# RWKV scan: the output weights' split ahead of the diagonals on GpSimd, the weights' rounding at the head's start on ScalarE

## The chip, the cores and the metric

The kernel runs on one core of one Trainium2 chip. The metric is the device time of one execution in microseconds (us). The engines are named as in the profile: PE is TensorE's matmul, PEld its weight load, DVE is VectorE, ACT is ScalarE, POOL is GpSimd, SP is SyncE, whose queue issues the loads and stores.

## What is computed

The program is a whole two-block network on 512 tokens of 1024 channels. The change lies in one part of it, the bidirectional RWKV scan of the second block, with 16 heads of 64 channels, over 256 context and 512 latent steps:

```
def _wkv_step(S, inp):
    r_t, w_t, k_t, v_t, a_t, b_t = inp
    sa = einsum('zbhvk,zbhk->zbhv', S, a_t)
    S = S * w_t[..., None, :] + sa[..., :, None] * b_t[..., None, :] + v_t[..., :, None] * k_t[..., None, :]
    return S, einsum('zbhvk,zbhk->zbhv', S, r_t)

def rwkv_out(y, h, xx, r, k_mod, v, mu, ln_g, ln_b, r_k, g1, g2, wo):
    y = layernorm(y, ln_g, ln_b, GN_EPS)                    # per head
    bonus = einsum('bthk,zbthk->bth', _heads(r) * r_k, _heads(k_mod))
    y = y + bonus[..., None] * _heads(v)
    gate = sigmoid(xg @ g1) @ g2
    return (y * gate) @ wo
```

Beside the scan proper, each head's turn of the program also does two small things for the stage that follows. It takes one 128x512 block of the output weights `wo` and splits it into a rounded part and the rest, so that the later product can be made of three products of rounded values. And it adds the bias `ln_b` of the head's 64 channels to the bonus rows (the offset).

## The kernel before, in words

`rwkv_scan` (L3304) works head by head, both directions at once, one in partitions 0 to 63 and one in 64 to 127. A head's 768 steps are cut into 12 chunks of 64 (`STEPS`), in three groups of four (`NG` = 3). Each engine has a hand-written program; `heads(body)` calls `body(h, walk, ahead)` for h = 0 to 15, in which three heads are in work at once:

- head h is *prepared*: PE multiplies the factors into pair products (`pair_set` 0 to 4, masked by DVE into `pairs`), turns the keys with the diagonals `eed` (`turn` 0 to 2, copied by ACT into `bkT`, L3560), and a triangular inverse R is grown in 15 steps (`NZ` = 15): for each n, PE makes z from `off[n]` and T, ACT copies it to Z (L3580), PE makes zr from Z and R, and DVE adds zr to R (L3737) and transposes R into T (L3706);
- head h-1 is *walked*: 12 steps, each of X (L3510), SA (L3514) and Sm (L3519), copied by ACT between PE's products; steps 0 to 2 lie at the start of the body, between pair products and turned keys, the others between the growth steps, and y is copied at the very end (L3507). `walk_solve`, PE's product of X and R, needs all 15 updates of R for step 0 and the copied X in each step;
- the *factors* of head h+1 are made, between the growth steps, by DVE (prefix scan L3624, `at_rt` L3655, `bh` L3661, `ee` L3677 at the twelfth step) and ACT, and by POOL.

**POOL** (L3456 on), in `body`: the three joins of R (L3477, after DVE's `scaled`), the fifteen `off` products (L3482), then `factors(ahead)`: `km` (L3461), `kh` (L3466, after ACT's exponential `e_neg`), the diagonals `eed` (L3468, after DVE's `ee`, semaphore `bd_ready`). Then the split `w_lo` = `w_raw` - `w_hi` (L3486, after ACT's rounding, `hi_made`) and the offset of the head before (`add_shift`, L3493).

**ACT**, in `body`: walk steps 0 and 1, the copies of the turned keys with walk step 2 between them, the copies of z with the rest of the walk and the exponentials of the factors. At n = `NZ` - 4 = 11 it rounds the weights' block, `w_hi` = `w_raw` (L3594), after `raw_loaded` (both loads of the block: 128x512 of the weights, L3421, and the head's 64 biases on 128 partitions into `shift`, L3422) and after the stores of the block before.

**DVE**, in `body`: masks, scales and eyes at the start, then the growth steps with the factor parts between them. Ahead of the last update of R (n = 14) stand the two bonus multiplies of `add_bonus` (L3726).

**SP**, in `body`: loads of the factors of the head ahead; then it waits for the copy of y of the walked head, loads v (L3415), waits for `bonus_done` and `lo_made`, stores `w_hi` and `w_lo` (L3438), waits for the offset of the head before and loads the next block's `w_raw` and `shift` (L3421, L3422):

```
                    if walk is not None:
                        sp.wait_ge(s["y_copied"], walk + 1)
                        if ahead is not None:
                            load_v(ahead)
                    sp.wait_ge(s["bonus_done"], h + 1)
                    sp.wait_ge(s["lo_made"], h + 1)
                    for d, w in zip(wo, (w_hi, w_lo)):
                        sp.dma_start(block_of(d, h), w[:].bitcast(F32)).then_inc(s["w_stored"], 16)
                    if ahead is not None:
                        if h:
                            sp.wait_ge(s["bonus_shifted"], h)
                        load_raw(ahead)
```

Of the kernel before, what the change touches and what calls it, by code (L numbers as in the profile page):

```python
# [10 lines left out]
ACT = mybir.ActivationFunctionType  # L11
# [3292 lines left out]
def rwkv_scan(nc, name, S, a, kF, rF, sgF, aF, vS, y, bonus_rows, wo):  # L3304

    NG = STEPS // 4
    NZ = LEVELS * NG
# [12 lines left out]
    with Stage(nc, name) as st:  # L3320
# [43 lines left out]
        s = {n: st.sem(n) for n in names}  # L3364
# [13 lines left out]
        def cs(x):  # L3378
            return x[:].rearrange("p (c t) -> p c t", t=CH)
# [7 lines left out]
        def heads(body):  # L3387
            for h in range(HEADS):
                body(h, h - 1 if h else None, h + 1 if h + 1 < HEADS else None)
# [6 lines left out]
        with st.block() as block:  # L3396
# [56 lines left out]
            def _(pool):  # L3453
                pool.wait_ge(s["const_loaded"], 96)

                def factors(h):  # L3456
# [7 lines left out]
                    if h:  # L3464
                        pool.wait_ge(s["tr_ready"], h * NG)
                    nc.gpsimd.tensor_tensor(kh[:], cs(km), cs(e_neg), ALU.mult).then_inc(s["kh_made"], 1)  # L3466
                    pool.wait_ge(s["bd_ready"], h + 1)
                    nc.gpsimd.tensor_tensor(eed[h % 3][:], eye[:].rearrange("p (o t) -> p o t", o=1).broadcast_to([P, STEPS - 1, CH]),  # L3468
                                            ee[h % 3][:, 0:STEPS - 1].rearrange("p (c o) -> p c o", o=1).broadcast_to([P, STEPS - 1, CH]), ALU.mult).then_inc(s["eed_made"], 1)

                def body(h, walk, ahead):
# [11 lines left out]
                    if ahead is not None:  # L3483
                        factors(ahead)
                    pool.wait_ge(s["hi_made"], h + 1)
                    nc.gpsimd.tensor_tensor(w_lo[:], w_raw[:], w_hi[:], ALU.subtract).then_inc(s["lo_made"], 1)  # L3486
                    if h:
                        add_shift(h - 1)

# [5 lines left out]

                factors(0)
                heads(body)
                add_shift(LAST)

            @block.scalar  # L3500
            def _(act):
# [47 lines left out]
                def body(h, walk, ahead):  # L3549
# [12 lines left out]
                    walk_both(0)  # L3562
                    walk_both(1)
                    copy_turned(0)
                    if walk is not None:
# [18 lines left out]
                    for n in range(NZ):  # L3584
                        if n + 1 < NZ:
                            copy_z(n + 1)
                        walk_part(walk, 2 * n)
                        walk_part(walk, 2 * n + 1)
                        if ahead is not None:
                            factor_part(ahead, n)  # L3590
                        if n == NZ - 4:
                            act.wait_ge(s["raw_loaded"], 32 * h + 32)
                            act.wait_ge(s["w_stored"], 32 * h)
                            A(w_hi[:], w_raw[:], ACT.Copy).then_inc(s["hi_made"], 1)  # L3594

# [946 lines left out]
```

## Time and profile before

| What | us |
|---|---|
| median of 3 runs | 4310.55 |
| their range | 4308.35 to 4314.49 |
| the profiled execution | 4311.74 |
| its span | 4309.8 |
| PE busy | 3577.5 (83%) |
| PEld busy | 2528.0 (59%) |
| DVE busy | 2089.9 (48%) |
| POOL busy | 1369.2 (32%) |
| ACT busy | 1244.6 (29%) |

The profiled execution is one run of the program under the hardware profiler. Its time is the device time, its span goes from the first to the last instruction. Busy time is the sum over the instructions of an engine, without waiting. The shares are those of the whole span; the scan is the part from about 2940 to 3640 us. In the lines of a timeline, the first number is the start, the second the duration, both in us, then engine, line of the program, operation, output and inputs, shapes and count; in brackets stands how long the engine was idle before, and what ended it. Instructions of one kind that follow each other are merged, and one may begin before the one ahead of it has ended. "issue" is time in which the engine waited for nothing that the profile shows.

### The profile page before, as it was taken

What the parts mean: (1) busy time and instruction counts of PE and PEld (TensorE: products, weight loads), DVE (VectorE), ACT (ScalarE), POOL (GpSimd) and SP (SyncE); (2) the same over time, 40 slices, a digit from 0 to 9 for tenths busy, and PEclk for the clock granted to TensorE, in tenths of its full rate; (3) what the DMA queues carried; (4) which work ended last, traced back from release to release, by engine and by line L of the source; (5) the groups of instructions that cost most, each with busy time, mean ns of one, the idle gap of its engine ahead of it and who ended that gap; (6) DMA issues with size and microseconds to landing.
All of it is one profiled execution on the core that took longest, in us unless ns stands there. A gap on an engine that the chain in (4) does not pass through costs nothing. (4 is left out here: it accounts for less than half of the span.)

```text
span 4309.8 us, 78120 instructions
## 1 busy us (share of the span) xinstructions
PE 3577.5 (83%) x31346; PEld 2528.0 (59%) x31346; DVE 2089.9 (48%) x3273; ACT 1244.6 (29%) x2681; POOL 1369.2 (32%) x1069
## 2 busy tenths in 40 slices
PE   8889999998999999968787848876888887587874
PEld 6667777556778887752222326635888886432221
DVE  4559963448983455640000036625878875400002
ACT  3352223443223223321111021223454443111112
POOL 4444453343443554720000023403455452000001
PEclk9999999999999999979898978997999997798997
DMA  4125532214542223449999963334223223599997
GB/s 125 47 79 178 182 133 79 63 50 150 181 161 76 98 74 120 146 179 420 421 421 421 421 244 108 125 134 130 67 64 78 53 78 113 210 394 426 426 426 298
DMA packets 245738, 819.09 MB, mean 190 GB/s; under 512 B 61336, under 2 KB 68840, under 8 KB 185680
## 3 DMA queue, kind: packets, MB, share of 16 engines
q1 hardware_dynamic: 236960, 786.13, 48.8%
q0 software_dynamic: 7920, 28.84, 1.7%
q8 instruction: 209, 3.42, 0.3%
q14 instruction: 73, 0.60, 0.0%
q10 hardware_dynamic: 576, 0.09, 0.0%
HBM read 738.84 MB, written 76.12 MB: 189 GB/s over the span
## 5 line engine op out<-in xcount | busy, mean ns | idle before, releaser
L2810 POOL DMA_INDIRECT moe0e_xg<-moe_h,moe_first_rows x19 | 18.0, 950 | 593.7 <-DMA moe_first_rows<-moe_table 544.0
L3758 PE MATMUL scan_bank<-scan_T,scan_off 64*64 64x64 f32 x3840 | 163.0, 223 | 43.5 <-issue 35.9
L1209 DVE SCALAR_TENSOR_TENSOR f0u_ada<-hT,condition,f0u_ada 128x512 f32<-128x512 f32 x168 | 196.9, 1242 | 0.2 <-DVE f0u_ada L1209 0.2
L1209 DVE SCALAR_TENSOR_TENSOR f1u_ada<-hT,condition,f1u_ada 128x512 f32<-128x512 f32 x168 | 191.2, 1207 | 0.2 <-DVE f1u_ada L1209 0.2
L2842 PE MATMUL moe0e_p_g<-moe_ring,moe0e_xT 128*64 128x512 f32 x608 | 175.1, 652 | 18.2 <-ACT moe0e_xT L2880 9.7
L2810 POOL DMA_INDIRECT moe1e_xg<-moe_h,moe_first_rows x16 | 15.1, 942 | 537.0 <-DMA moe_first_rows<-moe_table 454.9
L3482 POOL TENSOR_TENSOR scan_off<-scan_pairs,scan_join 128x256 f32<-128x256 f32 x240 | 181.3, 795 | 0.0
L359 POOL TENSOR_TENSOR gmi_w_lo<-gmi_rows_w,gmi_w_hi 128x512 fp32r<-128x512 f32 x64 | 120.5, 1883 | 161.6 <-ACT gmi_w_hi L399 161.6
L3758 PEld LDWEIGHTS scan_bank<-scan_T,scan_off 64*64 64x64 f32 x3840 | 140.2, 138 | 51.8 <-issue 42.8
L2842 PE MATMUL moe0e_p_u<-moe_ring,moe0e_xT 128*64 128x512 f32 x608 | 169.1, 631 | 0.0
L359 POOL TENSOR_TENSOR p_w_lo<-p_rows_w,p_w_hi 128x512 fp32r<-128x512 f32 (+3 forms) x88 | 113.4, 1290 | 163.0 <-ACT p_w_hi L399 163.0
L2909 DVE TENSOR_TENSOR moe0e_gated<-moe0e_gate,moe0e_p_u 128x512 f32<-128x512 f32 x19 | 13.1, 688 | 310.9 <-ACT moe0e_gate L2884 310.9
L3758 PE MATMUL scan_bank<-scan_R,scan_Z 64*64 64x64 f32 x3840 | 160.1, 221 | 1.8 <-issue 1.7
L1141 POOL TENSOR_TENSOR f1u_w_lo<-f1u_w,f1u_w_hi 128x1024 fp32r<-128x1024 f32 x42 | 115.5, 2769 | 136.4 <-ACT f1u_w_hi L1157 136.4
L2842 PE MATMUL moe1e_p_g<-moe_ring,moe1e_xT 128*64 128x512 f32 x512 | 145.9, 650 | 15.5 <-ACT moe1e_xT L2880 8.1
L1141 POOL TENSOR_TENSOR f0u_w_lo<-f0u_w,f0u_w_hi 128x1024 fp32r<-128x1024 f32 x42 | 114.0, 2735 | 138.2 <-ACT f0u_w_hi L1157 138.2
L2861 PE MATMUL moe0e_p_y<-moe_ring,moe0e_gatedT 128*64 128x512 f32 x608 | 140.9, 618 | 13.0 <-ACT moe0e_gatedT L2886 13.0
L3737 DVE TENSOR_TENSOR scan_R<-scan_R,scan_bank 128x256 f32<-128x256 f32 x240 | 98.2, 409 | 91.8 <-PE scan_bank L3758 90.7
L2842 PE MATMUL moe1e_p_u<-moe_ring,moe1e_xT 128*64 128x512 f32 x512 | 140.9, 630 | 0.0
L3758 PEld LDWEIGHTS scan_bank<-scan_R,scan_Z 64*64 64x64 f32 x3840 | 138.7, 137 | 2.4 <-issue 2.0
L2909 DVE TENSOR_TENSOR moe1e_gated<-moe1e_gate,moe1e_p_u 128x512 f32<-128x512 f32 x16 | 11.0, 688 | 261.0 <-ACT moe1e_gate L2884 261.0
L2861 PE MATMUL moe1e_p_y<-moe_ring,moe1e_gatedT 128*64 128x512 f32 x512 | 118.1, 615 | 11.0 <-ACT moe1e_gatedT L2886 11.0
(745 smaller groups left out, 10403.5 us busy)
## 6 DMA issues: line engine op xcount, KB each, us to landing
moe_ring<-in_moe_w_gu_dram SPq DMA_DIRECT2D x280, 1024.0 KB, 20.9
moe_ring<-in_moe_w_down_dram SPq DMA_DIRECT2D x140, 1024.0 KB, 22.6
hT<-in_ada_w_dram SPq DMA_DIRECT2D x48, 1024.0 KB, 6.6
f0u_w<-in_ffn_w_gate_up_dram SPq DMA_DIRECT2D x22, 1024.0 KB, 4.9
f1u_w<-in_ffn_w_gate_up_dram SPq DMA_DIRECT2D x22, 1024.0 KB, 4.8
gmi_rows_w<-in_ga_w_in_dram SPq DMA_DIRECT2D x64, 256.0 KB, 2.8
gmo_w<-in_ga_w_out_dram SPq DMA_DIRECT2D x64, 256.0 KB, 3.0
p_rows_w<-in_ab_w_in_dram SPq DMA_DIRECT2D x48, 256.0 KB, 2.7
```

Source lines behind the costliest of these rows:

```text
L359: nc.gpsimd.tensor_tensor(w_lo[t % 2][:, 0:width], w[t % RAW][:, 0:width], w_hi[t % 2][:, 0:width], ALU.subtract).then_inc(w_lo_made, 1)
L1141: nc.gpsimd.tensor_tensor(w_lo[u][:, g], w[:, g], w_hi[u][:, g], ALU.subtract).then_inc(lo_made, 1)
L1209: ins = V.scalar_tensor_tensor(out=acc[:, z, :], in0=src, scalar=cond[:, n * HALF + k, z:z + 1], in1=acc[:, z, :], op0=ALU.mult, op1=ALU.add)
L2810: pool.indirect_dma_start(xg[:], None, H.h, bass.IndirectOffsetOnAxis(rows[:, 0:1], 0)).then_inc(gathered, 16)
L2842: mm = nc.tensor.matmul(p[r, :], xT[:, kd, r], ring[:, s, half, k, g * HID:(g + 1) * HID], start=(kd == 0), stop=(kd == KD - 1), skip_grou ...
L2861: mm = nc.tensor.matmul(p_y[n][r, :], aT[:, kh, r], ring[:, s, half, k, n * BANK:(n + 1) * BANK], start=(kh == 0), stop=(kh == KH - 1), sk ...
L2909: nc.vector.tensor_tensor(act_in[:], sg[:], p_u[:], ALU.mult).then_inc(gated, 1)
L3482: nc.gpsimd.tensor_tensor(off[n][:], strict(u, g), over4(join[:, l + 1, :]), ALU.mult).then_inc(s["off_ready"], 1)
L3737: V.tensor_tensor(R[u][:, g4, :], R[u][:, g4, :], quad(zr_bank[n % 2]), ALU.add).then_inc(s["zr_added"], 1)
L3758: mm = nc.tensor.matmul(out[r], lhsT[r], rhs[r], start=start, stop=stop, skip_group_check=True)
```

## The change

On GpSimd, `factors` loses its last instruction, which becomes a function of its own, `diagonals`. In `body` the split and the offset now come right after `factors(ahead)`, and the diagonals after both. On ScalarE the rounding of the block, with its two waits, moves from the growth step n = 11 to the start of the body, behind walk steps 0 and 1 and ahead of the copies of the turned keys. No instruction is added or removed.

```diff
--- before.py
+++ after.py
@@ -3464,6 +3464,8 @@
                     if h:
                         pool.wait_ge(s["tr_ready"], h * NG)
                     nc.gpsimd.tensor_tensor(kh[:], cs(km), cs(e_neg), ALU.mult).then_inc(s["kh_made"], 1)
+
+                def diagonals(h):
                     pool.wait_ge(s["bd_ready"], h + 1)
                     nc.gpsimd.tensor_tensor(eed[h % 3][:], eye[:].rearrange("p (o t) -> p o t", o=1).broadcast_to([P, STEPS - 1, CH]),
                                             ee[h % 3][:, 0:STEPS - 1].rearrange("p (c o) -> p c o", o=1).broadcast_to([P, STEPS - 1, CH]), ALU.mult).then_inc(s["eed_made"], 1)
@@ -3482,10 +3484,15 @@
                         nc.gpsimd.tensor_tensor(off[n][:], strict(u, g), over4(join[:, l + 1, :]), ALU.mult).then_inc(s["off_ready"], 1)
                     if ahead is not None:
                         factors(ahead)
+                    split_block(h)
+                    if h:
+                        add_shift(h - 1)
+                    if ahead is not None:
+                        diagonals(ahead)
+
+                def split_block(h):
                     pool.wait_ge(s["hi_made"], h + 1)
                     nc.gpsimd.tensor_tensor(w_lo[:], w_raw[:], w_hi[:], ALU.subtract).then_inc(s["lo_made"], 1)
-                    if h:
-                        add_shift(h - 1)
 
                 def add_shift(h):
                     hs = slice(h * HK, h * HK + HK)
@@ -3494,6 +3501,7 @@
                                             shift[h % 2][:].rearrange("p (o c) -> p o c", o=1).broadcast_to([P, NT, HK]), ALU.add).then_inc(s["bonus_shifted"], 1)
 
                 factors(0)
+                diagonals(0)
                 heads(body)
                 add_shift(LAST)
 
@@ -3561,6 +3569,9 @@
 
                     walk_both(0)
                     walk_both(1)
+                    act.wait_ge(s["raw_loaded"], 32 * h + 32)
+                    act.wait_ge(s["w_stored"], 32 * h)
+                    A(w_hi[:], w_raw[:], ACT.Copy).then_inc(s["hi_made"], 1)
                     copy_turned(0)
                     if walk is not None:
                         walk_x(walk, 2)
@@ -3588,10 +3599,6 @@
                         walk_part(walk, 2 * n + 1)
                         if ahead is not None:
                             factor_part(ahead, n)
-                        if n == NZ - 4:
-                            act.wait_ge(s["raw_loaded"], 32 * h + 32)
-                            act.wait_ge(s["w_stored"], 32 * h)
-                            A(w_hi[:], w_raw[:], ACT.Copy).then_inc(s["hi_made"], 1)
 
                 act.wait_ge(s["const_loaded"], 96)
                 act.wait_ge(s["consts_made"], 2)
```

## Rows read from the trace of the kernel before

**Rows 1.** Stretches (us, busy of each engine with count, PEclk, DMA share, GB/s): scan, one head

```profile
core 0: us, PE busy (x) PEld busy (x) DVE busy (x) ACT busy (x) POOL busy (x), PEclk, DMA share, GB/s
2940.00:3640.00 700.00, 604.00 (x17728) 571.75 (x17728) 538.50 (x1075) 324.06 (x994) 336.09 (x369) 0.95 0.25 64
3248.73:3289.47 40.74, 36.23 (x1116) 34.45 (x1112) 33.84 (x68) 19.81 (x63) 21.19 (x23) 1.00 0.24 63
```

**Rows 2.** Timeline of PE near one head boundary (start us, us; in brackets idle before, releaser)

```profile
3235.45 0.68 PE L3758 MATMUL scan_bank<-scan_T,scan_off 64*64 64x64 f32 x16 [0.33 <-issue]
...
3243.11 0.33 PE L3758 MATMUL scan_bank<-scan_X,scan_R 64*64 64x64 f32 x4 [0.84 <-DVE scan_R L3737]
...
3250.36 0.31 PE L3758 MATMUL scan_bank<-scan_X,scan_R 64*64 64x64 f32 x4
```

**Rows 3.** Timeline of DVE, same stretch

```profile
3230.66 2.10 DVE L3655 SCALAR_TENSOR_TENSOR scan_at_rt<-scan_k,scan_negkk,scan_lw 128x384 f32<-128x384 f32 x1
...
3233.49 0.58 DVE L3655 SCALAR_TENSOR_TENSOR scan_at_rt<-scan_k,scan_negkk,scan_lw 128x384 f32<-128x384 f32 x1
3233.98 0.55 DVE L3661 TENSOR_TENSOR scan_bh<-scan_ka,scan_e_neg 128x384 f32<-128x384 f32 x1
...
3234.90 0.45 DVE L3706 STREAM_TRANSPOSE scan_T<-scan_R 128x256 f32<-128x256 f32 x1
...
3240.66 1.94 DVE L3726 TENSOR_TENSOR rw_bonus<-scan_v,scan_bonus 64x256 f32<-64x256 f32 x2
```

**Rows 4.** Instructions by tile over the kernel (ns min/median/max)

```profile
L3486 POOL TENSOR_TENSOR scan_w_lo<-scan_w_raw,scan_w_hi x16: 1267/1448/1452, 2990.3 to 3602.4; 128x512 fp32r<-128x512 f32 x16
...
L3726 DVE TENSOR_TENSOR rw_bonus<-scan_v,scan_bonus x32: 409/1050/1523, 2989.4 to 3605.0; 64x256 f32<-64x256 f32 x32
L3493 POOL TENSOR_TENSOR rw_bonus<-rw_bonus,scan_shift x16: 717/904/909, 3034.6 to 3605.5; 128x256 f32<-128x256 f32 x16
```

**Rows 5.** Timeline of POOL, same stretch

```profile
3230.52 1.82 POOL L3466 TENSOR_TENSOR scan_kh<-scan_km,scan_e_neg 128x768 f32<-128x768 f32 x1 [6.94 <-ACT scan_e_neg L3544]
3239.55 1.37 POOL L3468 TENSOR_TENSOR scan_eed<-scan_eye,scan_ee 128x704 f32<-128x704 f32 x1 [7.21 <-DVE scan_ee L3677]
3240.88 1.45 POOL L3486 TENSOR_TENSOR scan_w_lo<-scan_w_raw,scan_w_hi 128x512 fp32r<-128x512 f32 x1
3242.28 0.91 POOL L3493 TENSOR_TENSOR rw_bonus<-rw_bonus,scan_shift 128x256 f32<-128x256 f32 x1
3244.19 0.73 POOL L3477 TENSOR_TENSOR scan_R<-scan_pairs,scan_join 128x256 f32<-128x256 f32 x1 [1.00 <-DVE scan_pairs L3694]
```

**Rows 6.** Timeline of DVE in two heads, the prefix scan

```profile
3217.55 0.56 DVE L3624 TENSOR_TENSOR_SCAN scan_L<-scan_keep,scan_lw 128x192 f32<-128x192 f32 x1 [0.60 <-ACT scan_lw L3529]
...
3256.50 0.91 DVE L3624 TENSOR_TENSOR_SCAN scan_L<-scan_keep,scan_lw 128x192 f32<-128x192 f32 x1 [0.41 <-ACT scan_lw L3529]
```

**Rows 7.** Timeline of ACT, boundary of rows 2

```profile
3237.66 0.62 ACT L3594 ACTIVATE scan_w_hi<-scan_w_raw 128x512 fp32r<-128x512 f32 x1
...
3240.69 0.38 ACT L3507 ACTIVATE rw_y<-scan_bank 128x256 f32<-128x256 f32 x1 [0.43 <-PE scan_bank L3767]
...
3248.73 0.60 ACT L3560 ACTIVATE scan_bkT<-scan_bank 128x512 f32<-128x512 f32 x1 [0.71 <-PE scan_bank L3773]
```

**Rows 8.** Timeline of SyncE's queue, same boundary

```profile
3241.10 1.30 SPq L3415 DMA_DIRECT2D scan_v<-rw_v  x2
...
3244.09 0.64 SPq L3422 DMA_DIRECT2D scan_shift<-in_rw_ln_b_dram  x1
```

**Rows 9.** Landings by tile: shift over the kernel, shift here, w_raw over the kernel

```profile
DMA to landing us min/median/max: 4.4/5.2/6.7
...
DMA to landing us min/median/max: 6.3/6.3/6.3
...
DMA to landing us min/median/max: 3.4/3.8/5.3
```

**Rows 10.** Stretches of a head in which PE stood longer

```profile
3372.06:3413.98 41.92, 37.34 (x1116) 35.62 (x1112) 32.64 (x68) 20.04 (x63) 20.45 (x23) 0.96 0.29 76
3377.00:3381.00 4.00, 4.00 (x91) 4.00 (x89) 0.14 (x1) 1.69 (x6) 4.00 (x7) 0.57 0.37 96
```

**Rows 11.** Timeline of PE in that head

```profile
3376.12 0.22 PE L3849 MATMUL scan_bank<-ones,scan_rk 64*64 64x1 f32 x2 [1.67 <-issue]
```

## The prediction

> **What bounds the kernel now.** I read the stretch table first. The scan takes 700 us of the 4309.8 us span, and PE, the busiest engine, is busy for 604 of them; DVE is busy for 538.5, ACT and POOL for about half [rows 1]. No engine is full, so what counts is who waits for whom within one head, of which there are 16, some 41 us each. The profile's chain of work that ended last names only the tail of the kernel and is of no use here. I then read the timelines of all engines over one head boundary, 3230 to 3253 us, and those of the other boundaries, which repeat it.
>
> At the boundary, PE issues the product of X and R of the next walk (the first matmul that needs the last update of R) after standing 0.84 us for DVE's update of R [rows 2]. DVE is late with that update because two bonus multiplies lie in front of it and take 1.94 us together [rows 3]. The pair would need about 0.8 us (0.41 us is the shortest of the 32 [rows 4]); the rest is waiting, because POOL is at that moment in the diagonals (3239.55 to 3240.92), the split (to 3242.33) and the offset [rows 5]. A vector instruction with two SBUF operands ends only after the POOL instruction that is under way: the same shows beside POOL's kh, where DVE's first half of `at_rt` takes 2.10 us and the second half, with POOL idle, 0.58 us [rows 3, 5]. The prefix scan of 128x192 takes 0.56 us with POOL idle and 0.91 us beside the `off` products [rows 6].
>
> So the change has a real target: POOL's split and offset lie beside DVE's last two-operand work of a head, ahead of something that PE waits for.
>
> **The change, part by part.**
>
> 1. *The split and the offset leave the boundary.* They run 3240.88 to 3243.19 now [rows 5]. Without them the bonus multiplies wait for the diagonals alone, that is to about 3240.92, and end near 3241.5, 1.1 us earlier. PE can use only the 0.84 us that it stands [rows 2]. That is a gain of at most 0.84 us at each of 15 boundaries. POOL's next work, the joins of R, starts after waiting 1.00 us for DVE [rows 5], so POOL was not late for it and gains nothing of its own.
>
> 2. *They arrive right behind kh, at about 3232.3.* There POOL is idle now until 3239.55 [rows 5], so POOL's own time costs nothing, and the diagonals still wait for DVE's small product of decays. But DVE is not idle: it has the second half of `at_rt` (3233.49) and the first half of bh (3233.98), both with two SBUF operands, in between updates of R and transposes [rows 3]. When kh ends, DVE finishes the `at_rt` it was held in (3232.76), then the split runs some 1.27 us (its shortest, with DVE idle; 1.45 us beside DVE [rows 4, 5]) to about 3234.0. The second `at_rt` half is held to there and ends at 3234.45 instead of 3234.0. The offset, 0.7 us at its shortest [rows 4], runs to 3235.15, and bh, held again, ends about 1.05 us late. Behind it stand an update of R and the transpose of 3234.90. PE's growth step at 3235.45 starts 0.1 us after that transpose, having stood 0.33 us [rows 2, 3]. There is no slack there, and PE is then without a pause until the y products. I take +1.0 us a head. Bounds: 0.3 us if only the first hold counts and the second is hidden, 2.0 us (split plus offset, 1.27 + 0.7) if POOL keeps the memory over both.
>
> 3. *ScalarE's rounding leaves its old place.* There it took 0.52 us of ACT's queue (its 0.62 us, of which the next instruction overlaps some 0.1 us [rows 7]) and made the copies behind it at most some 0.15 us late. I take -0.1 us; bounds 0 and -0.5 us.
>
> 4. *The rounding in its new place waits for a load.* Only the timeline of SyncE's queue shows this term. ACT is ready for it at 3248.02: it stands 0.71 us there now, until the first turned keys come at 3248.73 [rows 7]. The rounding needs 0.5 us, so by its length alone it would fit. But it waits for both loads of its block, the weights and the offset's row. SyncE issues them at the end of a series that starts when y is copied (3240.69 to 3241.07): two loads of v, two stores of the block before, the weights' load, and at 3244.09 the load of `shift` [rows 7, 8]. That last one lands 5.2 us after its issue in the median (4.4 to 6.7 over 16), and 6.3 us in this head; the weights themselves take 3.8 us [rows 9]. So the rounding may start at 3249.3 (median) or 3250.4 (this head), 1.3 to 2.4 us after ACT is ready for it. Before, ACT asked for these loads some 30 us later, and they cost nothing. Nothing in this series becomes earlier: y's copy does not depend on the bonus, and the stores are at most a few tenths bound by it.
>
> Queued behind it on ACT are the copy of the turned keys and the copy of X of step 2. With 0.5 us for the rounding and 0.5 us for the copy, X is written at 3250.6 to 3251.7. PE takes X at 3250.36 today [rows 2]. So PE's walk is 0.3 to 1.4 us later than now, 0.85 us in the middle, even though the boundary ahead of it was 0.84 us quicker. The gain of part 1 is thus consumed: PE arrives early and stands, about 1.7 us in all.
>
> How much of 0.85 us reaches the end of the head? The profile has a natural experiment. In the head of 3372 us PE stood 1.67 us in the bonus matmuls and then ran at a granted clock of 0.57 for 4 us, half speed, together some 2.4 us of delay; that head took 41.92 us where one without such a stop took 40.74 [rows 1, 10, 11]. About half came through, since DVE then meets less of POOL's `off` work. I take 0.4 us. Bounds 0 and 1.4 us.
>
> **The sum.** 1.0 - 0.1 + 0.4 = 1.3 us a head, with part 1 already used up inside part 4. Times 15 it is 19.5 us. The first head has its load long before, and the last has no following head whose factors it prepares; neither matters. The profiled execution took 4311.74 us, 1.9 us more than its span and 1.2 us above the median of the three runs, 4310.55. So 4331 us.
>
> *A page against the rows.* The row says 5.2 us for the 32 KB of `shift` (64 floats on 128 partitions). The Trainium skill, DMA: Bandwidth & Descriptors, section on the anatomy of one DMA, fits a transfer as about 2.0 us fixed plus its bytes over 436 GB/s, an estimate by it of 2.1 us here. By that the row of `shift` would be there at 3246.2, ahead of ACT; the trace does not agree, and the trace's duration is used. The page's figure would lead to the faster rival below.
>
> **The rivals.**
>
> *Faster: the load is not what ACT waits for.* If the landing that ends the wait were at or before 3248.0, so if `shift` landed within 3.9 us of its issue, ACT's copy would move by nothing and the 0.84 us of part 1 would stay. With the holds of DVE hidden by PE's own work, 15 x 0.84 = 12.6 us are won: 4299 us. For it: the weights alone take 3.8 us. Against it: the smallest of 16 landings of `shift` is 4.4 us. It decides at 3.9 us.
>
> *About the same: the costs are the small ends.* Holds of 0.3 us and a wait that passes on 0.1 us come to 0.3 us a head, 5 us in all: 4316 us. For it: DVE does stand for PE at times, and a hold that falls on such a time is free. Against it: PE, not DVE, is the one without a pause from 3235.45 on, and a late start of its growth step is not made good.
>
> *Much slower: the clock.* PE stands about 1.7 us in part 4, as long as in the head of 3372 us, after which the granted clock was 0.57, which is the lower of its levels (1.2 of 2.4 GHz) for most of 4 us [rows 10, 11]. If that follows in most heads, another 1.2 us of half-speed work comes through: 2.5 us a head, 4349 us. Against it: over the whole scan the clock is 0.95 [rows 1], although PE stands at every boundary.
>
> *The change does not do what it says* is hardly open: the order of each queue is written by hand, and the diff moves whole instructions.
>
> **How the numbers follow.** The forecast has 0.60, the clock 0.15, the small ends 0.17, the faster one 0.08. A measurement of this kernel can tell about 0.2%, 8.6 us, from no change. Part of the small-end case reaches beyond 8.6 us. So faster 0.07, same 0.15, slower 0.78. The range from 4312 to 4349 takes in the small ends and the clock and leaves out the faster rival and what lies beyond the bounds.
>
> **What would show it.** In the changed kernel ACT should show an idle time of 2 to 3 us before the rounding, ended by a DMA, and PE an idle time of 1 to 2.5 us before the product of X and R of step 2, ended by ACT. DVE's bonus pair should fall from 1.9 to about 1.0 us, PE's 0.84 us before the first product of X and R should vanish, and DVE's second half of `at_rt` and first half of bh should grow from 0.58 and 0.55 to about 1.0 and 1.2 us. The period of a head should go from 41 to a little over 42 us. I would be wrong if ACT does not idle before the rounding, or if DVE's two instructions keep their length.

## The result and the profile after

The changed kernel takes 4320.93 us in the median of 15 runs (4314.45 to 4337.17). The kernel before, run beside it, takes 4310.09 us in the median of 15 (4299.87 to 4321.01). The ratio is 1.003, with a 95% interval of 1.0022 to 1.0038: slower by 12.9 us (9.5 to 16.4). The forecast was 20 us slower, a range from 4312 to 4349. The sign and the range hold, the size was too large. The profiled execution took 4318.85 us, with a span of 4317.0.

The stretch table of the changed kernel has the same columns as [rows 1]; its three rows are a long stretch of the scan, 4 us from the copy of X in one head boundary, and the 4 us behind those. The row below them, by itself, is the long stretch in the kernel before.

```profile
3000.00:3600.00 600.00, 528.46 (x15892) 505.35 (x15890) 465.52 (x954) 284.61 (x888) 298.78 (x329) 0.97 0.24 63
3497.00:3501.00 4.00, 3.67 (x72) 3.67 (x74) 0.16 (x1) 1.95 (x7) 4.00 (x7) 0.50 0.65 169
3501.00:3505.00 4.00, 4.00 (x108) 4.00 (x106) 0.88 (x3) 2.18 (x7) 3.77 (x6) 0.72 0.02 5
```

```profile
3000.00:3600.00 600.00, 532.75 (x16187) 507.46 (x16185) 478.47 (x962) 288.79 (x905) 303.13 (x337) 0.99 0.25 64
```

In the same 600 us the changed kernel gets through 954 instructions of DVE instead of 962. Its mean clock is 0.97 instead of 0.99, with stretches at 0.50, which is the lower level, 1.2 of 2.4 GHz. Taken from one copy of y to the next over 14 heads, a head takes 41.78 us instead of 40.82 us. Over the 13 of them that prepare a following head it is 42.02 us instead of 41.25 us.

**The granted clock over whole executions.** Every timed run has its span and its mean granted clock. The span times what the clock lacks to 1 is the lacking clock, the most that a full clock could have saved. The rest is what would be left of the span. The changed kernel's 15 runs have a mean clock of 0.9129, the 89 runs of the kernel before that were timed beside the experiments, on three chips, 0.9162. Against those 89, in means with 95% intervals, us:

| version | lacking clock | rest of the span |
|---|---|---|
| changed kernel | +15.5 ± 5.0 | -2.9 ± 3.9 |
| e1 | +6.6 ± 4.8 | -3.4 ± 2.5 |
| e4, both times | -9.7 ± 3.5 | -9.6 ± 3.3 |
| e5, both times | -2.2 ± 3.2 | -0.8 ± 2.5 |
| e6, both times | -8.3 ± 3.0 | -1.3 ± 2.8 |
| e7 | -10.4 ± 3.9 | -3.0 ± 3.9 |

So all of the changed kernel's loss lies in time at a lower granted clock, as far as these figures can tell. That is book-keeping and not yet a cause: what made the clock fall isn't in it. The experiments e1 to e7 are told below.

**The new wait.** Timeline of ScalarE in the changed kernel, a usual boundary and a bad one:

```profile
3075.72 0.63 ACT L3574 ACTIVATE scan_w_hi<-scan_w_raw 128x512 fp32r<-128x512 f32 x1 [1.89 <-DMA scan_shift<-in_rw_ln_b_dram]
3076.26 0.58 ACT L3568 ACTIVATE scan_bkT<-scan_bank 128x512 f32<-128x512 f32 x1
3076.73 0.22 ACT L3518 ACTIVATE scan_X<-scan_bank 128x64 f32<-128x64 f32 x1
...
3496.05 0.63 ACT L3574 ACTIVATE scan_w_hi<-scan_w_raw 128x512 fp32r<-128x512 f32 x1 [3.65 <-DMA scan_shift<-in_rw_ln_b_dram]
...
3497.06 0.22 ACT L3518 ACTIVATE scan_X<-scan_bank 128x64 f32<-128x64 f32 x1
```

ScalarE stands before the rounding, ended by a load, and the copies of the turned keys and of X come behind it, where [rows 7] has the turned keys at once. Timeline of PE, the same two boundaries, the first line being the first product of X and R:

```profile
3068.46 0.31 PE L3765 MATMUL scan_bank<-scan_X,scan_R 64*64 64x64 f32 x4
...
3077.00 0.27 PE L3765 MATMUL scan_bank<-scan_X,scan_R 64*64 64x64 f32 x2 [0.69 <-ACT scan_X L3518]
...
3497.33 0.37 PE L3765 MATMUL scan_bank<-scan_X,scan_R 64*64 64x64 f32 x2 [1.82 <-ACT scan_X L3518]
```

The stand of [rows 2] before the first product, which DVE ended, is gone (no bracket); a new one, ended by ScalarE, stands 8.5 us later. The waits of the whole scan say it in sums: who waited, for what, us, times, longest. First the changed kernel, then the kernel before:

```profile
ACT scan_w_hi L3574 <- DMA scan_shift<-in_rw_ln_b_dram: 41.6, 15, 4.8
PE scan_bank L3765 <- ACT scan_X L3518: 23.5, 14, 3.6
PE scan_bank L3765 <- DVE scan_R L3744: 1.4, 2, 0.7
```

```profile
PE scan_bank L3758 <- DVE scan_R L3737: 15.1, 16, 1.7
```

**DVE.** Timelines of DVE and POOL in the changed kernel, growth part and boundary:

```profile
3097.32 2.14 DVE L3662 SCALAR_TENSOR_TENSOR scan_at_rt<-scan_k,scan_negkk,scan_lw 128x384 f32<-128x384 f32 x1
3099.38 0.41 DVE L3744 TENSOR_TENSOR scan_R<-scan_R,scan_bank 128x256 f32<-128x256 f32 x1
...
3100.19 0.81 DVE L3662 SCALAR_TENSOR_TENSOR scan_at_rt<-scan_k,scan_negkk,scan_lw 128x384 f32<-128x384 f32 x1
3100.92 1.08 DVE L3668 TENSOR_TENSOR scan_bh<-scan_ka,scan_e_neg 128x384 f32<-128x384 f32 x1
...
3107.95 0.96 DVE L3733 TENSOR_TENSOR rw_bonus<-scan_v,scan_bonus 64x256 f32<-64x256 f32 x2
```

```profile
3097.24 1.81 POOL L3466 TENSOR_TENSOR scan_kh<-scan_km,scan_e_neg 128x768 f32<-128x768 f32 x1 [8.25 <-ACT scan_e_neg L3552]
3099.01 1.57 POOL L3495 TENSOR_TENSOR scan_w_lo<-scan_w_raw,scan_w_hi 128x512 fp32r<-128x512 f32 x1
3100.55 1.04 POOL L3500 TENSOR_TENSOR rw_bonus<-rw_bonus,scan_shift 128x256 f32<-128x256 f32 x1
3106.82 1.36 POOL L3470 TENSOR_TENSOR scan_eed<-scan_eye,scan_ee 128x704 f32<-128x704 f32 x1 [5.24 <-DVE scan_ee L3684]
```

Against [rows 3] the second half of `at_rt` grew from 0.58 to 0.81 us and the first half of bh from 0.55 to 1.08 us; the bonus pair fell from 1.94 to 0.96 us. The updates of R, which read PSUM, keep their 0.41 us beside the split and beside kh alike.

What the holds do to PE can be read too. Behind the held bh stand an update of R and a transpose, and PE's next growth step starts as the transpose ends. The same step in the changed kernel (two lines) and in the kernel before:

```profile
3102.37 0.45 DVE L3713 STREAM_TRANSPOSE scan_T<-scan_R 128x256 f32<-128x256 f32 x1
3102.91 0.68 PE L3765 MATMUL scan_bank<-scan_T,scan_off 64*64 64x64 f32 x16 [1.28 <-issue]
```

```profile
3276.37 0.68 PE L3758 MATMUL scan_bank<-scan_T,scan_off 64*64 64x64 f32 x16 [0.51 <-issue]
```

The profile puts this stand down to "issue", but the matmul reads the T that the transpose writes, and it starts 0.09 us after the transpose has ended, so it is DVE that ends it. In the mean of 13 heads it is 1.26 us in the changed kernel and 0.50 us in the kernel before: the holds reach PE with 0.76 us a head, which is their own length.

### The profile page after: what moved, and what is told of

It reads as the page before. It is cut to its first block and busy times, and to the rows that moved or that the text cites. A ratio compares the mean times of both kernels' runs of the same rounds, so it can differ in the third digit from the quotient of the medians.

```text
span 4317.0 us, 78120 instructions
## 1 busy us (share of the span) xinstructions
PE 3577.1 (83%) x31346; PEld 2533.6 (59%) x31346; DVE 2077.1 (48%) x3273; ACT 1245.1 (29%) x2681; POOL 1366.1 (32%) x1069
## 5 line engine op out<-in xcount | busy, mean ns | idle before, releaser
L1209 DVE SCALAR_TENSOR_TENSOR f1u_ada<-hT,condition,f1u_ada 128x512 f32<-128x512 f32 x168 | 178.8, 1132 | 2.2 <-DMA hT<-in_ada_w_dram 1.9
L2842 PE MATMUL moe1e_p_g<-moe_ring,moe1e_xT 128*64 128x512 f32 x512 | 147.0, 655 | 15.5 <-ACT moe1e_xT L2880 8.1
L2861 PE MATMUL moe1e_p_y<-moe_ring,moe1e_gatedT 128*64 128x512 f32 x512 | 118.3, 616 | 11.0 <-ACT moe1e_gatedT L2886 10.3
```

The source lines that it names most:

```text
L1209: ins = V.scalar_tensor_tensor(out=acc[:, z, :], in0=src, scalar=cond[:, n * HALF + k, z:z + 1], in1=acc[:, z, :], op0=ALU.mult, op1=ALU.add)
L2842: mm = nc.tensor.matmul(p[r, :], xT[:, kd, r], ring[:, s, half, k, g * HID:(g + 1) * HID], start=(kd == 0), stop=(kd == KD - 1), skip_grou ...
L2861: mm = nc.tensor.matmul(p_y[n][r, :], aT[:, kh, r], ring[:, s, half, k, n * BANK:(n + 1) * BANK], start=(kh == 0), stop=(kh == KH - 1), sk ...
```

## The experiments

Each was timed against the kernel before on the same chip. Ratios have their 95% intervals, and a microsecond figure from a ratio is the ratio's distance from 1 times 4310.

**e1: the rounding alone is moved.** From the kernel before:

```diff
                     walk_both(1)
+                    act.wait_ge(s["raw_loaded"], 32 * h + 32)
+                    act.wait_ge(s["w_stored"], 32 * h)
+                    A(w_hi[:], w_raw[:], ACT.Copy).then_inc(s["hi_made"], 1)
                     copy_turned(0)
...
-                        if n == NZ - 4:
-                            act.wait_ge(s["raw_loaded"], 32 * h + 32)
-                            act.wait_ge(s["w_stored"], 32 * h)
-                            A(w_hi[:], w_raw[:], ACT.Copy).then_inc(s["hi_made"], 1)
```

> Only ScalarE's half of the change: the rounding of the block at the start of the head, GpSimd's order as before. Theory (the rounding waits for the row of shift, which SyncE issues late): ACT idles 1.5 to 3 us before the rounding, ended by the load of shift; PE stands 0.5 to 1.5 us before the product of X and R of step 2; DVE's bonus pair stays at 1.9 us and the halves of at_rt and bh at 0.58 and 0.55 us; 0.3 to 0.5 us a head, so 5 to 8 us above the kernel before (ratio 1.001 to 1.002). Rival (the whole loss is DVE held beside the moved split and offset, and the wait of ACT is covered by PE's own queue): ratio 1.000 or below.

Measured 4314.19 us, ratio 1.0011 (0.9997 to 1.0024): +4.7 us, an interval that has 1 in it. Its waits over the scan:

```profile
ACT scan_w_hi L3566 <- DMA scan_shift<-in_rw_ln_b_dram: 32.2, 15, 4.6
PE scan_bank L3757 <- ACT scan_X L3510: 14.1, 13, 3.4
PE scan_bank L3757 <- DVE scan_R L3736: 13.5, 15, 1.7
```

The wait for the load is there and PE stands for it, and DVE's late update of R stays beside it. The middle value, 4.7 us, is a third of the 12.9 us and what the prediction had for parts 3 and 4 (-1.5 and +6), but the interval goes from -1.3 to 10.3 us, so this run alone doesn't say that the wait is the smaller part. The profiled execution was the fastest of the twelve (4306.96 us).

**e2: GpSimd's order alone is changed,** the rounding stays at n = 11 (the changed kernel with the last hunk of the diff undone).

> Only GpSimd's half: split and offset ahead of the diagonals, the rounding in its old place at n = 11. The split then waits for the rounding and runs near n = 12, so it holds DVE's rk multiplies by some tenths and pushes the diagonals by about 1 to 2 us, whose end then meets the bonus pair. Theory: no wait of ACT for a load, no hold of at_rt and bh; bonus pair 1.3 to 1.9 us; ratio 0.999 to 1.001. Rival (a split and an offset cost DVE the same anywhere in the growth steps, about 1 us a head): ratio 1.003.

Measured 4308.86 us, ratio 1.0001 (0.999 to 1.0013). Timeline of its POOL:

```profile
3070.13 1.27 POOL L3495 TENSOR_TENSOR scan_w_lo<-scan_w_raw,scan_w_hi 128x512 fp32r<-128x512 f32 x1 [6.02 <-ACT scan_w_hi L3602]
3071.36 0.91 POOL L3500 TENSOR_TENSOR rw_bonus<-rw_bonus,scan_shift 128x256 f32<-128x256 f32 x1
3072.37 1.36 POOL L3470 TENSOR_TENSOR scan_eed<-scan_eye,scan_ee 128x704 f32<-128x704 f32 x1
```

The split waits 6.02 us for the rounding, so it leaves the place behind kh and stands ahead of the diagonals, which it pushes into the bonus pair (1.86 us). GpSimd's half needs ScalarE's half, and this run can't price the holds behind kh.

**e3: the rounding waits for the weights alone.** The load of `shift` gets a semaphore of its own, for which the offset waits:

```diff
-                    act.wait_ge(s["raw_loaded"], 32 * h + 32)
+                    act.wait_ge(s["raw_loaded"], 16 * h + 16)
```

> The changed kernel with a semaphore of its own for shift: the rounding waits for the weights' load alone, the offset for the row. Theory: the weights land 3.8 us after an issue that is 0.5 us earlier, so the rounding starts about 2 us earlier than in the changed kernel; ACT's wait before it falls from 2.8 us to about 1 us, PE's stand before X and R of step 2 to a few tenths; the holds of DVE stay (0.23 and 0.53 us). 6 to 10 us below the changed kernel: ratio to the kernel before 1.0005 to 1.0015. Rival (holds alone): as slow as the changed kernel, 1.003.

Measured 4323.2 us, ratio 1.0032 (1.0021 to 1.0044). My theory's number (1.0005 to 1.0015) failed. The waits of this run, and its answer by tile for the weights' load (issue to landing, minimum, median, maximum):

```profile
ACT scan_w_hi L3575 <- DMA scan_w_raw<-in_rw_wo_dram: 32.9, 14, 3.8
PE scan_bank L3766 <- ACT scan_X L3519: 16.0, 12, 2.6
```

```profile
DMA to landing us min/median/max: 4.1/5.1/6.4
```

The weights land 5.1 us after their issue, not 3.8 us as [rows 9] have it. There, both loads counted up one semaphore, and the profile gives the first 16 counts to the first load, whichever load they came from. The Trainium skill, DMA: Bandwidth & Descriptors, section on why a DMA increments its semaphore by 16, says that the counts of two such loads in flight fill each other's; this run agrees, with 5.1 us against 3.8. The mistake was mine: 3.8 us was never the weights' landing. In this trace the weights have landed 8.4 us after the copy of y in the mean and the row of `shift` 9.3 us, so ScalarE's wait became shorter by half a microsecond (2.35 us against 2.89 us in the mean of 13 heads), and the time shows nothing of it.

**e4: split and offset between the joins.** From the kernel before; the rounding stays where it was, and the split and the offset of a block go behind the first and the second join of the next body, where DVE reads PSUM. For that, SyncE stores the block and loads the next one in the body that follows, ahead of its wait for y's copy.

```diff
                         nc.gpsimd.tensor_tensor(R[u][:, 4 * g:4 * g + 4, :], strict(u, g), over4(join[:, 0, :]), ALU.mult).then_inc(s["r_joined"], 1)
+                        if h and g == 0:
+                            split_block(h - 1)
+                        if h and g == 1:
+                            add_shift(h - 1)
...
                     if walk is not None:
+                        store_block(walk)
+                        load_raw(h)
                         sp.wait_ge(s["y_copied"], walk + 1)
```

> From the kernel before: the rounding stays at n = 11, but split and offset of a block run one head later, between GpSimd's joins of R, where GpSimd stands 1.6 us twice for DVE and DVE works from PSUM; the stores and the next block's loads follow there, so that the rounding has them some 20 us ahead. Theory: the bonus pair falls to about 0.9 us, PE's stand of 0.84 us before the first X and R goes, at_rt and bh keep 0.58 and 0.55 us, no wait of ACT for a load: 0.4 to 0.8 us a head gained, ratio 0.997 to 0.9985. Rival (the joins become late, since each gap is hardly longer than the split of 1.27 to 1.45 us, and with them R and the first transposes): ratio 1.000 to 1.003.

Measured 4291.94 us, ratio 0.9957 (0.994 to 0.9973); again on another chip 4291.53 us, 0.9955 (0.994 to 0.997). Both are faster than the 0.997 to 0.9985 that I expected. This version beats both kernels: 19 us less than before, and so some 32 us less than the changed kernel (19 + 12.9). Timeline of its POOL between the joins, then the line on PE's wait for R among its waits:

```profile
3192.33 0.73 POOL L3480 TENSOR_TENSOR scan_R<-scan_pairs,scan_join 128x256 f32<-128x256 f32 x1 [2.71 <-DVE scan_pairs L3703]
3193.02 1.27 POOL L3496 TENSOR_TENSOR scan_w_lo<-scan_w_raw,scan_w_hi 128x512 fp32r<-128x512 f32 x1
3194.65 0.73 POOL L3480 TENSOR_TENSOR scan_R<-scan_pairs,scan_join 128x256 f32<-128x256 f32 x1 [0.36 <-DVE scan_pairs L3703]
3195.34 0.72 POOL L3501 TENSOR_TENSOR rw_bonus<-rw_bonus,scan_shift 128x256 f32<-128x256 f32 x1
```

```profile
PE scan_bank L3767 <- DVE scan_R L3746: 1.4, 2, 0.7
```

Both instructions take their shortest times, 1.27 and 0.72 us, in gaps in which POOL waited for DVE anyway, and neither `at_rt`'s second half (0.50 us) nor bh's first (0.55 us) is held by them.

**e5: the loads ahead of y's copy.** From the changed kernel, SyncE's stores and the block's loads go ahead of the wait for y's copy:

```diff
+                    sp.wait_ge(s["lo_made"], h + 1)
+                    for d, w in zip(wo, (w_hi, w_lo)):
+                        sp.dma_start(block_of(d, h), w[:].bitcast(F32)).then_inc(s["w_stored"], 16)
+                    if ahead is not None:
...
+                        load_raw(ahead)
                     if walk is not None:
                         sp.wait_ge(s["y_copied"], walk + 1)
```

> The changed kernel with SyncE's part moved: the stores of the block and the loads of the next one are issued as soon as the split is done, ahead of the wait for y, some 15 us before the rounding needs them. Theory (two terms: the wait for the loads, and the holds of DVE): ACT does not wait for a load any more, the turned keys are copied 7.0 to 7.5 us after y instead of 9.9, PE's stand before X and R of step 2 is gone; the holds stay (at_rt 2.95, bh 1.60 us a head). The period falls from 41.8 to about 40.6 us (the 40.8 of the kernel before, less 0.9 of the boundary, plus 0.75 of the holds); ratio to the kernel before 0.998 to 1.000. Rival (the wait is covered by other queues, the holds are the loss): ratio 1.002 to 1.003.

Measured 4310.82 us, ratio 0.9998 (0.9986 to 1.001), and again 4307.05 us, 0.9991 (0.9981 to 1.0001). SyncE asks for the load at 3067.24 and not after the copy of y (at 3075.33 in this trace); ScalarE shows no wait for it, and PE none for X. The holds on DVE stay (`at_rt` 2.94 us, bh 1.60 us, the sums of two halves in a head, as in the changed kernel). With the wait gone the kernel stands where before stood, so what the wait and SyncE's order cost together is the changed kernel's 12.9 us less e5's -2.4 us (the mean of two), 15.3 us.

**e6: e4's order on SyncE, split and offset left at the boundary.** Against e4, whose two calls between the joins go:

```diff
                         factors(ahead)
+                    split_block(h)
+                    if h:
+                        add_shift(h - 1)
```

> Control for the version between the joins: the same new order of SyncE's stores and loads and the same deferral of them by a head, but split and offset on GpSimd at the boundary, as in the kernel before. Theory (the gain of that version is the freed bonus pair): the pair stays at 1.9 us, PE's stand before the first X and R at 0.8 us, ratio 0.999 to 1.001. Rival (the gain comes from moving the DMAs away from the loads of v): ratio 0.996 to 0.998.

Measured 4303.82 us, ratio 0.998 (0.9968 to 0.9992), and again 4301.79 us, 0.9979 (0.9968 to 0.9989). The expectation was missed: SyncE's order alone wins some 9 us. The boundary is as it was (PE stands for R 13.9 us in 15 times, the bonus pair takes 1.97 us), so those 9 us have another place. By the table of clocks they are time at a lower granted clock (-8.3 us, against -1.3 us of all else), and in the traces the 13 heads have a clock below 1.00 in three heads before, in none in e6 and in one in its repetition. The longest wait of ScalarE for the turned keys is 3.9 us before and 1.7 us in e6.

**e7: e5 with the offset behind the second join;** the split stays behind kh.

```diff
+                        if h and g == 1:
+                            add_shift(h - 1)
...
                     split_block(h)
-                    if h:
-                        add_shift(h - 1)
```

> As the version with the loads ahead of y, but the offset alone goes into GpSimd's gap behind the second join of R; the split stays behind kh. Theory: the hold of bh (0.53 us) goes, that of at_rt (0.2 to 0.3 us) stays; 0.3 to 0.5 us a head less than with both behind kh, 5 to 8 us, ratio 0.9965 to 0.9985. Rival (PE's growth step does not follow DVE there): no difference between the two.

Measured 4298.7 us, ratio 0.9969 (0.9958 to 0.9981). The answer by tile for bh on DVE (count, ns minimum, median and maximum), first e5, then e7:

```profile
L3668 DVE TENSOR_TENSOR scan_bh<-scan_ka,scan_e_neg x32: 515/544/1079, 2953.5 to 3559.5; 128x384 f32<-128x384 f32 x32
```

```profile
L3668 DVE TENSOR_TENSOR scan_bh<-scan_ka,scan_e_neg x32: 515/544/547, 2949.7 to 3554.8; 128x384 f32<-128x384 f32 x32
```

One hold of 0.53 us a head is away, and the time falls by 11 us (e5's mean ratio 0.99945 less 0.9969), 0.73 us a head with an uncertainty of some 0.35 us. PE's stand behind bh falls from 1.27 us (e5) to 0.73 us, by the length of the hold, so PE pays the hold on bh in full. What is measured beyond it is within the noise, and by the table of clocks most of the difference between e5 and e7 is lacking clock.

**f1: a wait put back.** e5, with one more wait ahead of the rounding, for the load of `sg` that SyncE issues behind y's copy:

```diff
                     act.wait_ge(s["raw_loaded"], 32 * h + 32)
+                    if ahead is not None:
+                        act.wait_ge(s["sg_loaded"], 32 * ahead + 32)
```

> The version with the loads ahead of y, in which the rounding waits in addition for the load of sg of the head ahead, which SyncE issues right behind v at the boundary and which lands some 8 to 9 us after y's copy. No transfer moves; only the wait of ScalarE comes back. Theory (the wait itself costs, through the late copy of X): ACT idles 1 to 2.5 us before the rounding, PE stands 0.5 to 1.5 us before X and R of step 2; 4 to 10 us above the version without it, ratio to the kernel before 1.001 to 1.002. Rival (the changed kernel's loss beside the holds is the crowd of transfers at the boundary and not the wait): equal to the version without it, 0.9998.

Measured 4307.84 us, ratio 0.9993 (0.9984 to 1.0002), no different from e5. Its waits:

```profile
ACT scan_w_hi L3576 <- DMA scan_sg<-rw_sg: 18.3, 13, 2.2
PE scan_bank L3767 <- ACT scan_X L3518: 3.3, 6, 1.0
```

The expected 4 to 10 us didn't come, and the number is the rival's. A wait of 1.4 us in the mean (18.3 over 13) cost nothing that can be measured: PE stood for X in six heads only, 3.3 us in all. The clock over 3000 to 3600 us is 0.99 in this trace, as before. The changed kernel's wait is 2.8 us in the mean (41.6 over 15), so f1 has only half the dose. It doesn't decide whether the rest of the wait costs, or the transfers at the boundary, which e5 and f1 both lack.

**f2: more transfers.** The kernel before, with two further copies of 256 KB from memory to memory issued behind the load of `shift`. It asks whether e6's gain is less crowding of the DMA at the boundary.

```diff
                         load_raw(ahead)
+                        for n in range(2):
+                            sp.dma_start(spare[n][:, :], block_of(a["rw_wo_2"], h)).then_inc(s["spare_loaded"], 16)
```

> The kernel before with two more transfers of 256 KB behind the load of shift at each boundary (a block of weights to a spare place in DRAM; nothing reads it). Theory (the new order of SyncE gained 8.6 us because fewer transfers are under way when PE needs its next instructions): PE's idle times put down to issue near the turned keys grow in number and length, and the kernel is 5 us or more slower, ratio 1.001 to 1.004. Rival (the gain came from SyncE issuing the factors' loads 2 us earlier, or was chance): the extra transfers delay the factors' loads by 1 us and no more happens, 1.000.

Measured 4312.12 us, ratio 1.0001 (0.999 to 1.0012). The 512 KB copied more at that place cost nothing clear of some 5 us. But the trace has a part of what the theory asked for: the 13 heads took 542.9 us against 536.3 us before, PE's stands put down to issue 46.4 us against 39.8 us, and six heads had a clock below 1.00 instead of three. The timed runs and the one trace pull apart here, so crowding is unlikely to explain e6 and isn't ruled out.

## Why the prediction was right in sign and range, and too large

The differences between timed versions, each uncertain by some 5 us, stand beside the terms of the sum. e5 and e4 differ in SyncE's order and in the rounding's place too, so the first row is the holds only as far as these cost nothing, and the third row is not measured by itself: it is what is left of the sum, uncertain by some 6 us:

| term | predicted, us | from the runs, us |
|---|---|---|
| holds on DVE behind kh (parts 2 and 3) | +15.0 - 1.5 | +16.6, e5 less e4 (means of two ratios) |
| boundary free of split and offset (part 1) | -12.6, but used up in part 4 | -10.1, e4 less e6 |
| rounding waits for the load (part 4) | +6, after it took up part 1 | +6.4, the rest; e1 alone +4.7 |
| together | +19.5 | +12.9 |

*Part 1, the boundary.* Right. The bonus pair went from 1.94 to 0.96 us, PE's stand for R from 15.1 us in 16 times to 1.4 us in 2.

*Part 2, the holds.* Right in kind, and **mis-sized: the first term of the sum, 1.0 us a head, measured 0.76 us.** The two holds sum to 0.23 + 0.53 = 0.76 us, where I had 1.05, and PE's stand behind them grew by the same 0.76 us. That is 11.4 us over 15 heads instead of 15. The order on POOL was as predicted; the second half of `at_rt` was held for less, because it starts only after an update of R and a transpose, when the split has little left. By the timed runs e7 has the hold on bh alone at 11 us, and e4 against e7 the rest at 5.6 us. Their sum, 1.1 us a head, is 0.3 us more than the 0.76 us, about as much as it is uncertain. The Trainium skill, SBUF — State Buffer, section on the two separate sides, says that GpSimd and a vector instruction with two SBUF inputs take one pair of ports in turn, each for its whole instruction; the traces agree (bh from 0.55 to 1.08 us beside the offset, updates of R from PSUM unchanged at 0.41 us).

*Part 3.* e2 moves nothing on ScalarE and e1 has both places in it, so this term was not measured by itself; it is too small for these intervals.

*Part 4, the wait.* The wait came as described: 2.8 us in the mean where I had 1.3 to 2.4 us plus the idle 0.71 us of before. To see what became of part 1's gain, I count from the end of y's copy, which sets off the loads, to the moment when PE takes up the product of X and R of step 2. Means of the 13 heads that prepare a following one, us, one execution each:

```
                 PE takes X of step 2   from there to the next y   the head
before                  9.37                    31.88               41.25
e5, no wait             8.46                    32.43               40.89
e1, wait alone         10.53                    30.82               41.35
changed kernel         10.29                    31.72               42.02
```

Without the wait, the free boundary brings PE there 0.91 us earlier (e5), as part 1 has it. With the wait it comes 0.92 us later than before, where I had 0.85, and about as late in e1, whose boundary isn't free, as in the changed kernel. So "the gain of part 1 is thus consumed" holds at this place. The timed differences alone would say otherwise: the changed kernel less the holds leaves -4 us, where my sum had +6. But that rests on four versions and is uncertain by about 7 us, and it takes the holds at 16.6 us, while PE's stands have them at 11.4.

**The other mis-sized term is the share of the delay that reaches the end of the head.** I took half, 0.4 us. In the changed kernel a head is 0.77 us longer than before, no more than the holds alone would make it; in e1, in its fastest execution, it is 0.10 us longer for a delay of 1.16 us. The timed e1 (+4.7 us, -1.3 to 10.3) allows 0.4 us as well as nothing.

My half came from a wrong comparison. I set the head with the stop of 1.67 us [rows 11] against the head of 40.74 us as one without such a stop. That head has one of its own, later:

```profile
3264.53 0.68 PE L3758 MATMUL scan_bank<-scan_T,scan_off 64*64 64x64 f32 x16 [1.70 <-issue]
```

Besides, the delay itself was added up wrongly: 1.67 us and 4 us at a clock of 0.57 are 3.4 us, not 2.4. The heads of the kernel before with a clock of 1.00 take 39.74 to 41.77 us among themselves, so a difference of 1.2 us between two heads shows nothing.

Such a stand of 1.3 to 1.7 us, some 24 us after y's copy, is in 8 of the 13 heads before, and in 7 of the changed kernel, but in none of the five in which ScalarE waited longest. PE that comes late finds it gone. That is a likely reason why little of the delay comes through; no run tried it by itself.

*The last head.* "Neither matters" was wrong for this execution. The 14th head, which prepares no following one, took 38.73 us instead of 35.15 us, 3.6 us of the 13.5 us that its 14 heads lost in all. In the other traces it takes 33.85 to 36.52 us.

*The page on transfers.* The fit that the prediction quotes from the Trainium skill, DMA: Bandwidth & Descriptors, section on the anatomy of one DMA, is given there for transfers that GpSimd issues, and SyncE issues this one. So its 2.1 us was no estimate of this load, and 5.2 us in the trace is no contradiction to it.

*The clock rival* came in large part, and my sum had hardly anything for it. In the changed kernel's trace 6 of 13 heads have a granted clock below 1.00 (0.88 to 0.96), before it is 3 (0.92 to 0.96), and over all timed runs the loss is lacking clock (+15.5 us) and nothing else. Over the 13 heads of the two traces the lacking clock is 18.8 us against 6.8 us, while all stands of PE together are 60.6 us against 56.3 us. So the new stands, 21.4 us for X and 9.9 us behind bh, took the place of others: 11.9 us for R, the rest put down to "issue" or small. A head's 0.77 us equals the holds by its number, and not because PE stood that much longer. That a forecast made up of holds and a late walk came within 7 us of the measured loss is therefore partly luck. In the 13 heads of the changed kernel that prepare a following one, from one copy of y to the next (3026.15 to 3572.34 us), ScalarE's wait and the time of the head go like this:

```
ScalarE's wait, us   heads   PE's stand for X, us, sum   mean time of a head, us
1.42 to 2.88         8       8.4 (0.22 to 1.69)         41.33
3.47 to 4.83         5       12.9 (1.82 to 3.63)        43.11
```

Head by head against the kernel before, the five with the long wait lost 6.8 us and the eight others 3.1 us. Not all of it is the wait: the fifth head, 42.97 us here, took 43.30 us before with no such wait, after a stand of PE of 2.79 us for which the profile shows no cause. The 14th, at 3572.34 us, prepares no following head, has no kh and so none of the holds behind it. ScalarE's and PE's timelines in it, and its stretches (the whole head, then the 4 us from 3584 us); behind them the same head of the kernel before:

```profile
3582.01 0.63 ACT L3574 ACTIVATE scan_w_hi<-scan_w_raw 128x512 fp32r<-128x512 f32 x1 [3.31 <-DMA scan_shift<-in_rw_ln_b_dram]
...
3583.29 0.27 PE L3765 MATMUL scan_bank<-scan_X,scan_R 64*64 64x64 f32 x2 [2.11 <-ACT scan_X L3518]
...
3572.34:3611.07 38.73, 35.38 (x1068) 34.09 (x1065) 19.82 (x46) 15.89 (x55) 15.06 (x21) 0.96 0.13 35
3584.00:3588.00 4.00, 3.96 (x92) 3.96 (x94) 0.14 (x1) 1.73 (x7) 4.00 (x7) 0.65 0.01 4
```

```profile
3569.44:3604.59 35.15, 33.83 (x1068) 32.65 (x1065) 20.56 (x46) 15.79 (x56) 17.32 (x23) 1.00 0.14 38
```

The same 1068 matmuls take 3.58 us more: PE stands 2.11 us for X and then, in the 4 us from 3584 us, has a granted clock of 0.65, while the kernel before has 1.00 over the whole head. PE takes up the product of X and R 1.36 us later than before, and 4 us at 0.65 lack another 1.4 us. So long waits came with more loss than short ones: nothing measurable at 1.4 us in the mean (f1), more than PE's stop in this head, where it is 3.3 us. Each of these is one execution, and that the stop causes the low clock was not tried by itself.

*What would show it* held in kind at each point: ScalarE idle 1.4 to 4.8 us (2.8 in the mean), PE idle 0.2 to 3.6 us (1.6 in the mean), the pair at 0.96 us, 0.81 and 1.08 us for the two halves, less than my 1.0 and 1.2. The period went from 41.25 to 42.02 us in the heads that prepare a following one.

**Open.** Why SyncE's later order of stores and loads brings a higher granted clock, and 9 us (e6), is not settled; f2's added traffic cost nothing clear. The 15.3 us between the changed kernel and e5 are wait and SyncE's order together. Taking e6's 8.9 us off leaves 6.4 us, which is the third row of the table again and no second measurement of it. How the loss at the lower clock divides between the wait, the holds and the transfers at the boundary stays open.

## What to carry to other kernels

Before moving work of GpSimd, list what DVE does at the new place: beside instructions that read PSUM it is free, beside those with two SBUF inputs DVE pays (here 0.76 us a head, all of which PE stood for). When an instruction moves, its waits move with it: look at when the transfer is asked for, not only at the instruction's length, and give loads semaphores of their own before their landing times are believed. Whether a gain survives a wait behind it is read from when the work behind the wait starts, counted from what sets off the load. A head that is to serve as the undisturbed case has to be looked through for stands of its own. And the mean granted clock of all timed runs belongs beside their times: here it held the whole difference.

## What was not expected of the hardware

The whole loss of the changed kernel, +15.5 us ± 5.0, and nearly the whole gain of e6, -8.3 us ± 3.0, are differences in lacking clock. Waits of ScalarE of 3.3 us and more come with a lower clock behind them (0.50 in the 4 us from 3497 us, 0.65 in those from 3584 us), a wait of 1.4 us in the mean costs nothing measurable (f1). A stand of PE that the profile puts down to "issue" can be the trace of an instruction held on DVE: 1.26 us with both holds, 0.73 us with one (e7), 0.50 us with none. The order in which SyncE issues the same transfers was worth 9 us, twice, with the boundary unchanged.
